# Output projection of a hybrid attention/mLSTM decoder step in two passes over token halves, with three smaller reorderings

## What is computed

```python
for l in range(2):
    xn = rmsnorm(x, n1) * (1 + sc1) + sh1
    z = xn @ w_in                          # 1024 x 3128: queries, keys, values, gates
    # attention group: compressed blocks, selected blocks, window; mixed by gates
    # mLSTM group: chunkwise; forget gates are summed along the tokens (cumsum)
    b = cumsum(log_sigmoid(f), axis=tokens)
    C_new = decay * C + sum_s(ws * k * v)  # state of each of the 8 requests
    x = x + g1 * (concat(a_out, m_out) @ w_out)     # output projection, 1024 x 1024
    xn2 = rmsnorm(x, n2) * (1 + sc2) + sh2          # mean of squares over the 1024 features
    u, gt = split(xn2 @ w_up)                       # up projection, 1024 x 5632
    x = x + g2 * ((silu(conv3(u)) * gt) @ w_down)
y = rmsnorm(x, final_g)
```

## Time and profile before

| | us |
|---|---|
| median of three runs | 1756.97 |
| profiled execution, its device time | 1754.99 |
| its span, first to last instruction | 1753.1 |
| TensorE matmul busy | 1662.7 (95%) |
| VectorE busy | 918.9 (52%) |
| ScalarE busy | 610.3 (35%) |
| POOL busy | 176.7 (10%) |
| granted TensorE clock, mean | 0.966 of full speed |

### The profile page before, as it was taken

The page is one execution under the profiler, slowest core; times in us unless marked ns, Lnnn a source line. Parts: engine busy times, 40 slices in busy tenths (PEclk is TensorE's granted clock), DMA queues, the critical chain, the costliest instruction groups (busy, mean ns, idle before and its releaser), DMA issues.

```text
span 1753.1 us, 36993 instructions
## 1 busy us (share of the span) xinstructions
PE 1662.7 (95%) x14687; PEld 1505.4 (86%) x14687; DVE 918.9 (52%) x2381; ACT 610.3 (35%) x1164; POOL 176.7 (10%) x284
## 2 busy tenths in 40 slices
PE   5999999988999999999989999999898999999998
PEld 4999975557899999999979997655698999999997
DVE  2544445657275645546473453475636555645544
ACT  2322236634152413314152222564414331413314
POOL 1011004422010000000001101153201000000001
PEclk9899999998999999999999999999898999999999
DMA  9326297359242313221123444733854322312201
GB/s 347 117 78 184 68 335 252 115 187 186 98 144 72 105 66 97 97 84 61 52 80 94 155 149 171 257 106 106 192 95 144 97 97 82 103 59 95 97 25 57
DMA packets 156542, 219.40 MB, mean 125 GB/s; under 512 B 11467, under 2 KB 116363, under 8 KB 155933
## 3 DMA queue, kind: packets, MB, share of 16 engines
q1 hardware_dynamic: 151488, 201.45, 36.5%
q0 software_dynamic: 4896, 15.71, 3.4%
HBM read 208.77 MB, written 16.68 MB: 129 GB/s over the span
## 4 chain that ended last, share of the span: by engine, by line
PE 88%; DVE 5%; ACT 3%; DMA 1%; issue 1%; DVEq 1%; POOL 1%; SPq 0%; ACTq 0%
PE ps L1314 29%; PE ps L1387 15%; PE ps L858 13%; PE ps L1274 6%; PE ps L706 2%; PE ps L983 2%; PE ps L998 2%; PE ps L909 2%; PE ps L954 1%; PE ps L844 1%; PE ps L1103 1%; DMA big<-in_w_mod 1%; PE ps L853 1%; PE ps L852 1%; PE ps L1294 1%
## 5 line engine op out<-in xcount | busy, mean ns | idle before, releaser
L1314 PE MATMUL ps<-work_r,big_r 128*128 128x272 f32 x1344 | 279.2, 289 | 1.4 <-ACT work L1754 0.4
L1314 PE MATMUL ps<-work_r,slab_r 128*128 128x272 f32 x1344 | 278.5, 288 | 0.0
L1314 PE MATMUL ps<-xnT_r,big_r 128*128 128x272 f32 x1344 | 276.4, 287 | 0.0
L858 PE MATMUL ps<-slab_r,work_r 128*128 128x256 f32 (+1 forms) x976 | 213.7, 286 | 0.0
L1314 PEld LDWEIGHTS ps<-work_r,big_r 128*128 128x128 f32 x1344 | 210.1, 188 | 3.9 <-issue 3.9
L1314 PEld LDWEIGHTS ps<-xnT_r,big_r 128*128 128x128 f32 x1344 | 211.7, 188 | 0.0
L1314 PEld LDWEIGHTS ps<-work_r,slab_r 128*128 128x128 f32 x1344 | 210.5, 188 | 0.0
L1883 DVE TENSOR_TENSOR slab_r<-slab,big_r 128x2048 fp32r<-128x2048 f32 (+1 forms) x84 | 170.1, 2035 | 48.3 <-ACT big_r L1738 44.2
L858 PEld LDWEIGHTS ps<-slab_r,work_r 128*128 128x128 f32 x976 | 163.8, 192 | 2.7 <-issue 2.5
L1757 ACT ACTIVATE big<-big,work 128x560 f32<-128x560 f32 x44 | 33.6, 765 | 371.9 <-DVE big L2504 371.9
L1387 PE MATMUL ps<-side_r,big_r 128*128 128x272 f32 x696 | 145.7, 291 | 0.9 <-DVE big_r L1883 0.9
(11 more groups left out here) (474 smaller groups left out, 3156.2 us busy)
## 6 DMA issues: line engine op xcount, KB each, us to landing
slab<-in_w_mod SPq DMA_DIRECT2D x22, 2048.0 KB, 10.5
slab<-in_w_up SPq DMA_DIRECT2D x44, 1024.0 KB, 6.8
slab<-in_w_in SPq DMA_DIRECT2D x20, 1024.0 KB, 5.5
slab<-in_w_down SPq DMA_DIRECT2D x20, 1024.0 KB, 6.6
slab<-in_cache_cmp_kv SPq DMA_DIRECT2D x128, 128.0 KB, 2.1
slab<-in_cache_sel_kv SPq DMA_DIRECT2D x96, 128.0 KB, 2.0
big<-in_cache_win_kv SPq DMA_DIRECT2D x16, 512.0 KB, 7.0
out<-in_cache_win_kv POOLq DMA_DIRECT2D x16, 508.0 KB
```

The costliest lines, as they stand in the source:

```text
L858: ins = mm(ps[n % 4][:, 0:cw], x, fr(wt[:, k, :]), start=k == 0 and m == 0, stop=k == KC - 1 and m == 2)
L1314: ins = mm(ps[2 * half + b][:, 0:HALF], wt, fr(x[:, k, HALF * b:HALF * b + HALF]), start=k == 0 and n == 0, stop=k == KC - 1 and n == 2)
```

## The change

It has four parts.

**The output projection runs in two passes.** The first pass (h = 0) takes token columns 272 to 543 (240 prompt tokens and the 32 decode tokens) for all 8 output blocks, the second (h = 1) columns 0 to 271. One block of one pass is 24 matmuls into one bank; five banks are used in turn. The number of large matmuls and of weight loads stays the same: 384 in a layer. The sums of squares, the root, the reciprocal, the spread, the scaling and the splits are made for each half apart. Those of the first half stand beside the products of the second pass. `up_first` takes the first half's 48 matmuls, with the second half's last sum and its spread between them, and then the second half's 48. The high and low part of the second half's inputs, and of the weights, are spread over the first pass. The first two splits of up weights now stand before the end of the projection. The squares moved to another buffer, the turned conv history to another bank, and slab 0 is freed in the second pass.

**The gate sums** are four matmuls, of 16, 12, 8 and 4 columns.

**The stacking** loops over the kinds, and inside over the heads.

**The decay product** stands after `combine(1)`, and the scaled heads before the first two `state_added`.

```diff
+        OUT_BANKS = 5
+        HALVES = (slice(HALF, TT), slice(0, HALF))
+        TOKENS = (slice(HALF, SEQ), slice(0, HALF))
+        NH4 = HALF // 4
...
+            def half_sum(m, k, h, frees=None):
+                pe.wait_ge(*act_at(m, "square", k, h))
+                if k == 0 and h:
+                    pe.wait_ge(*dve_at(m, "var", 0, 0))
+                for q in range(4):
+                    ins = mm(ps[6][32 * q:32 * q + 32, 0:NH4], ones[:, 0:32], sqh[:, k % 2, NH4 * q:NH4 * q + NH4], start=k == 0,
+                             stop=k == KC - 1, tile_position=(0, 32 * q), skip_group_check=True)
...
-                    for t in range(PT_):
-                        for i in range(t + 1):
-                            mm(ps[4][:, MH * t:MH * t + MH], ones if i < t else tri[:, :], lf[:, i, :], start=i == 0, stop=i == t)
+                    for d in range(PT_):
+                        mm(ps[4][:, MH * d:MH * PT_], ones if d else tri[:, :],
+                           lf[:, 0:PT_ - d, :].rearrange("p t h -> p (t h)"), start=d == 0, stop=d == PT_ - 1, skip_group_check=True)
...
+                stacked(0, 4, lambda h: (idn(TS), RT[0:TS, 4, :, h]))
+                stacked(32, TS, lambda h: (oh[0:MH, h, 0:TS], G_s[:, 0, :]))
+                stacked(64, VA, lambda h: (idn(TS), proj_s[:, C_MV + VA * h:C_MV + VA * h + VA]))
+                stacked(256, DV, lambda h: (idn(TS), proj_s[:, C_MO + DV * h:C_MO + DV * h + DV]))
+                ins = stacked(384, TS, pair_rows)
...
+                mid = 2 * L + 1
+                for h in range(2):
+                    for c in range(8):
+                        i, n_ = c // 4, 8 * h + c
+                        if h == 0:
+                            pe.wait_ge(d_lo.sem, d_lo.at(c + 1, L))
+                        if n_ >= OUT_BANKS:
+                            pe.wait_ge(o_add.sem, o_add.at(n_ - OUT_BANKS + 1, L))
+                        if n_ == 8:
+                            pe.wait_ge(x_lo.sem, x_lo.at(X_OUT + 2 * KC, L))
...
+                        for k in range(KC):
+                            if n_ == 0:
+                                pe.wait_ge(x_lo.sem, x_lo.at(X_OUT + k + 1, L))
+                            wh, wl = fr(hiO[i][:, k, cc:cc + 128]), fr(lo[:, k, cc:cc + 128])
+                            for n, (wt, x) in enumerate(((wh, hiX), (wh, xnT), (wl, hiX))):
+                                ins = mm(ps[n_ % OUT_BANKS][:, 0:HALF], wt, fr(x[:, k, HALVES[h]]), start=k == 0 and n == 0,
+                                         stop=k == KC - 1 and n == 2)
...
+                        if h == 0:
+                            for k in ((), (), (0,), (1, 2), (3,), (4,), (5,), (6,))[c]:
+                                half_sum(mid, k, 0)
+                        elif c == 0:
+                            half_sum(mid, KC - 1, 0)
+                        else:
+                            half_sum(mid, c - 1, 1, frees=1 if c == 7 else None)
+                        if n_ == 9:
+                            half_spread(mid, 0)
...
+                    for h in range(2):
+                        b = 1 - h
+                        if h == 0:
+                            pe.wait_ge(o_add.sem, o_add.at(14, L))
+                            pe.wait_ge(x_lo.sem, x_lo.at(X_N2_DEC, L))
+                        for k in range(KC):
+                            if h:
+                                pe.wait_ge(x_lo.sem, x_lo.at(x_n2(k, 1), L))
...
+                            if h == 0 and k == 2:
+                                half_sum(mid, KC - 1, 1)
+                            if h == 0 and k == 5:
+                                half_spread(mid, 1)
...
-                tt(Cs[:, :, :, :], Cs[:, :, :, :], bc(decay[:, :, :], 3, VA), ALU.mult)
...
                 combine(1)
-                state_added(0)
-                state_added(1)
+                tt(Cs[:, :, :, :], Cs[:, :, :, :], bc(decay[:, :, :], 3, VA), ALU.mult)
+                drain()
                 dve.wait_ge(hs_root.sem, hs_root.at(1, L))
...
                 ts_(nd[:, 0:DV], Vst[:, 0:DV], hd[:, 3:4], None, ALU.mult).then_inc(ms_hd.sem, 1)
+                state_added(0)
+                state_added(1)
...
+                for c in range(8):
+                    dve.wait_ge(o_acc.sem, o_acc.at(8 + c + 1, L))
+                    residual_half(c, ps[(8 + c) % OUT_BANKS], 16 + c, 1).then_inc(o_add.sem, 1)
+                    if c == 0:
+                        half_var(mid, 0)
+                        half_inverse(mid, 0)
+                    for k in ((), (0, 1, 2), (3, 4, 5), (6, 7), (), (), (), ())[c]:
+                        half_scaled(mid, k, 0)
+                    for k in ((), (0, 1), (2, 3, 4), (5, 6, 7), (), (), (), ())[c]:
+                        half_low(k, 0)
...
+                    if c in (5, 7):
+                        split_w(c // 2 - 2, c // 2 - 2)
...
+                half_var(mid, 1)
+                half_inverse(mid, 1)
+                for k in range(KC + 1):
+                    if k < KC:
+                        half_scaled(mid, k, 1)
+                    if k:
+                        half_low(k - 1, 1)
```

225 lines of the change are left out of this document (149 added, 76 removed).

## The result

The changed kernel takes 1737.01 us (median of 4 runs, 1733.22 to 1739.98), the kernel before in the same session 1757.2. The ratio is 0.9894, with a 95% interval from 0.9867 to 0.9921. The forecast was 1733 within 1724 to 1744. The forecast was subtracted from the profiled execution of before (1754.99), so its like is 1733.22; between the medians the kernel gained less.

What follows compares the result with a forecast made beforehand. The prediction took TensorE, busy for 95% of the span, to bound the kernel. Its terms, 13.7 + 2.6 + 3.4 + 5.0 - 1.4 - 1.0 = 22.3 us off 1754.99, gave 1733, within 1724 to 1744.

Steps and rivals of the forecast that it cites:

- Two passes: Output projection to next up chunk: norm hidden beside products, gaining 7.0 us in layer 0 and 6.7 in layer 1.
- the spreads: Norm behind the output projection: both halves' spreads, with two changeovers and the decode piece, take 1.5 us a layer.
- The signs named: Behind the projection no TensorE idle over 1 us, clock 1.00; wrong: clock below 1 in passes, window-page wait over 1.5 us.
- rival 1: The clock falls behind gate sums and stacking stay, so 3.4 and 3.0 us are missing: 1739; chance 0.14.
- rival 2: The second half's norm comes back as a TensorE wait with slow clock; passes win 2 us a layer: 1743; chance 0.10.
- rival 3: Small sums drag the output projection to half clock: 1773 at 20 us of such products a layer; chance 0.04.
- rival 4: ScalarE or VectorE are late for most blocks of pass one, by 1 us each: 16 us, 1749; chance 0.04.
- Rival 5: ScalarE's table load ahead of the next chunk brings a drain with it: 2.8 us more, 1735.5; chance 0.06.
- Gate sums: Four wide matmuls take 0.85 us, winning 2.6 us of work; no clock fall behind them wins 3.4, both layers together.
- Stacking: Ordering by kind takes 1.3 us instead of 3.41; window-page DMA limits the gain to 2.5 a layer, 5.0 in all.
- Decay product: Decode tail: the moved product makes `state_added` come later, costing 0.7 us a layer, 1.4 in all.
- The clock ahead of the projection: TensorE idles longer there, so the slow clock can last into the projection: a loss of 0.5 a layer, 1.0 in all.

Runs made afterwards that it cites:

- up_late: The changed kernel with the first up weights issued only when the projection's second weight slab has landed; layer 1's passes took 75.59 us instead of 76.64.
- passes: The changed kernel with gate sums, stacking and decay product as before, so the two passes alone; 1745.95 us, ratio 0.9932 to the kernel before.
- again: The changed kernel measured once more, unaltered, on the chip of the runs with one part each; 1737.6 us, ratio 0.9891 to the kernel before.
- gates: The kernel before with only the gate sums changed, to four wide products; 1749.44 us, ratio 0.9961 to the kernel before.
- stack: The kernel before with only the stacking changed, ordered by kind; 1749.91 us, ratio 0.9968 to the kernel before.
- w_first: The changed kernel with the first four window pages issued ahead of the 16 late selected pages; 1740.16 us, ratio 0.9921 to the kernel before.
- d_early: The changed kernel with the decay product and first two additions in the old order; 8.54 and 8.20 us from numerator's copy to last state sums.
- fill: The changed kernel with 20 unread transposes ahead of the last state sums and 10 ahead of the projection; 1730.49 us, ratio 0.9866 to the kernel before.
- best: The changed kernel with paired half sums, late up weights, halved decay product, and unread transposes in decode tail and layer-end norm; 1728.51 us, ratio 0.9837.

## Why the prediction was right

**Two passes: 13.7 forecast, 10.3 in the profiled execution** (6.3 and 4.0). Layer 0 is 74.6 for 74. From 418.61 to 443.15 stand 168 products and 9 half sums in 24.54 us; less 168 x 0.1263 that is 3.3 us, 0.37 for a sum with its changeover (0.415 for a place, one of which has two). Taken the same way up to 471.85, with the first spread and the history off, the 16 sums of the layer are 6.6 us, 0.41 each, for 6.7. The term that was too small is the spreads: 1.01 + 0.22 + 0.85 = 2.1 us for 1.5. The forecast took both halves together as one whole spread (1.05) with two changeovers and the decode piece, but each half alone cost 0.85 to 1.01. The other misses are at the end. With T = 466.43, the last sum ends at T + 3.0 (3.1), the spread at T + 6.3 (6.1), the second half begins at T + 7.95 (7.6), its products end at T + 14.3 (13.8) and the next chunk begins at T + 15.2 (14.5). VectorE's steps of 0.82 a block pace the second half, as forecast, but they start later; by these steps alone the forecast's wait of 0.2 would be 0.3, and it measured 0.4. Layer 1 is where the term was mis-sized: 76.6. The half clock lies on 5.6 us of the first pass instead of 2.8, 1.4 us more, and 0.6 us is a wait for the second weight slab. The forecast took layer 1's gain as that of layer 0 and never asked when that slab lands; in up_late, where the up weights behind it on the same queue were held back, it landed 18.9 us after its issue instead of 25.3. In layer 1 of passes, with no such wait and a shorter half clock on the first pass, the stretch took 74.6.

**The signs named.** Behind the projection TensorE had no idle time over 0.6 us and the clock stayed at 1.00 in both layers of the profile after. Two signs of being wrong came up in other traces. In layer 1 of again the clock fell once more inside the passes (80.1 us, 2.6 of it waiting for the slab). And the wait for DMA at the window pages, 0.7 and 1.4 us in the profile after, was over the 1.5 us named in 7 of the 20 stretches with the new order, up to 2.1.

**The rivals.** The median of 1737 lies between the forecast's 1733 and the 1739 of rival 1, so the time does not decide between them. The traces do in part: the fall behind the gate sums went, but half clock came back elsewhere (layer 0 of gates), so rival 1 has some truth. Rivals 2, 3 and 4 are out by the profile after: TensorE did not wait at the spreads, the passes stood at 1.00 from 411, and pass one had no wait on the splits behind its first product.

**The rule on the table load** (the Trainium skill, ScalarE: Activation LUTs, section What ACT_TABLE_LOAD costs) asked for a drain of some 1.4 us with each. The trace does not agree: the load runs from 479.41 for 1.28 us, and the copy starts at 480.73, just as the sums are there. Rival 5 is out.

**Gate sums: 2.6 + 3.4 forecast.** The work is right (0.79 for 0.85, 1.3 us a layer), and the fall behind the sums is gone in every run that has them wide: it begins within 4 us of the sums in all six stretches with the old ones and in none of the 22 with the new ones. Against the rule of the Trainium skill that lays falls to idle gaps (TensorE: Matmul & The Clock Gate, section Why this matters for your kernels), TensorE was busy for 10.00 of 10.00 us with the fall and without. What it is worth is less certain. From the gate sums to the first late issue, the profiled executions with the old sums (before, stack, passes) average 290.7 and 285.5 us in the two layers, the 11 with the new ones 287.4 and 280.0. That is 8.8 us for both layers, 2.6 of it work, where the forecast had 6.0; with three traces on one side and this scatter it is uncertain by about as much as the part of the clock. But the single ones reach from 276.9 to 293.2, and go with the time at half clock in the stretch: 0 to 27 us by the granted clock. In the pair shown first, layer 0 gained 8.2 and layer 1 0.1, so the table's 8.2 is partly luck, and so is the 0.1.

**Stacking: 5.0 forecast, some 3.2 measured.** The sums gained 2.5 us a layer, more than the 2.1 of the forecast, and what is late next is the DMA, as forecast. From the first late issue to the copy the six stretches with the old order average 40.0 us, the 20 with the new order (w_first left out) 38.4: 1.6 a layer. The turn of keys ahead of the window keys takes 2.23 us where nothing is late; with the new order 2.2 to 3.7, mostly near 3. The forecast had two limits for this, 1.7 us by the median landing and 4.8 by the fastest, and took 2.5; the lower one, the row that stood for the usual case, was the better number. w_first shows that the transfers bind in the other order too.

**Decay product: -1.4 forecast, -1.0 in the profiled pair** (0.33 and 0.66), and between 0 and 0.3 a layer against d_early. The direction was right, and so was the step itself: the last state sums begin 0.65 us later behind the copy, for 0.7. The wait it made, 2.60 us, is where the clock falls in the pair shown; d_early has the fall as well (a stretch of 17.1 us from 400.2), so the product does not cause it.

**The clock ahead of the projection, -1.0 forecast:** nothing in layer 0 and 1.4 us in layer 1, which are counted in the 10.3 us of the passes above. Right in sum, wrong in taking both layers as one.

The 22.3 us of the forecast stand against 21.7 for the pair of profiled executions, and 20.2 (this pair) and 17.6 (again) between the medians. In that pair the passes with their clock gave 10.3 (12.7 forecast), the stretches behind the gate sums 8.3 (6.0), the stacking 4.4 (5.0), the decay product -1.0 (-1.4), and the stretches that the change doesn't touch -0.4. In these a loss of 1.0 us stands at the norm that ends layer 0, where the half clock lasted 10.2 us instead of 6.8 and the spread took 2.11 us instead of 1.43; the forecast had nothing for it. The sum was closer than its terms: what the passes lacked, falls of the clock elsewhere made up in that execution. That part is luck.

## What to carry to other kernels

Where a norm stands behind a large product, cut the tokens into halves and let the norm of one half run beside the products of the other: it cost 16 x 0.4 us of small sums and won 4 to 6 us of 20 a layer, and 0.5 where a weight slab came late and the clock fell once more (layer 1 of again). Take such sums in pairs, and look at when each weight slab of the doubled loop lands, since it landed 6 us later here with other transfers queued behind it. Once TensorE is busy throughout, the granted clock is the next thing to read: idle waits of 2 us filled with transposes may be worth a quarter to a third of this change (fill, not told from chance), and they should fit the wait at either clock, as those of best did not.

## What the runs showed of the hardware

- The clock can fall with no or little idle time ahead: in the stretch of the earlier trace rows, and in fill at 407.2, with TensorE busy for 4.00 of 4.00 and then 3.73 of 4.00 us before it. It stayed up in waits of 2 to 3 us when these were filled. No single cause that I tried explains all falls.
- The same program varies with these falls. Mean granted clocks of 0.974 to 0.980 in six runs of the changed kernel go with 1740.96 to 1734.81 us.
- Matmuls of a few columns cost by their order. 20 of them whose neighbours go to the same column tile took 3.41 us, and 0.9 us when neighbours alternate between the tiles and equal shapes stand together.
- A half sum or a spread of half the columns does not take half the time: 0.26 us for 0.37, and 0.85 to 1.01 for 1.16 (the whole spread at full clock in best).
- Of eight window pages of 512 KB behind 16 selected ones of 128 KB the fourth, which the chain waits for, landed 6.2 to 8.4 us after its issue, and with four of them issued first TensorE waited 4.65 us for the selected ones.
